# Modulation weights by contraction chunks, products slot by slot, and the vector tables ahead of the weight ring

## The chip, the cores and the metric

The kernel runs on one core of a Trainium2 chip. The metric is the time of one execution on the device, in microseconds (us). Five engines work side by side, each on its own list of instructions: TensorE (PE; its weight loads are shown as PEld), VectorE (DVE), ScalarE (ACT), GpSimd (POOL) and SyncE (SP). They meet at semaphores. SP and ACT also issue DMA transfers; in the profile SP's transfers stand under queue q1 and ACT's under q10, and both are carried out by the same 16 DMA engines.

## What is computed

One inference step of a two-layer backbone for two groups of 128 tokens (g = 0, 1), all in float32. Cut to what bears on the change:

```python
def _modulation(cond, w, b):              # w: 1024 x 6144
    m = jax.nn.silu(cond) @ w + b
    return jnp.split(m[:, None, :], 6, axis=-1)
...
for l in range(DEPTH):                    # DEPTH = 2
    sh1, sc1, g1, sh2, sc2, g2 = _modulation(cond, p['ada_w'], p['ada_b'])
    h = _rmsnorm(x, norm1) * (1 + sc1) + sh1
    proj = h @ p['w_in']                  # input projection, 3232 columns
    ...                                   # three mixer branches, merge, output projection
    x = x + g1 * mix
    x = x + g2 * _moe(_modulate(x, norm2, sh2, sc2), p)   # 32 experts, top 4
```

The condition has two rows, one for each group of tokens, so the modulation is a product of 2 rows with a 1024 x 6144 matrix in each layer.

## The kernel before

**The ring.** The weights of a layer's front (everything ahead of the experts) are packed on the host into 32 positions of up to 128 partitions x 4096 float32 (2 MB). Position `pos` is loaded into ring slot `pos % 6`. Positions 0 to 5 of layer 0 are loaded by `load_early` in a setup block, those of layer 1 at the end of layer 0. All others are loaded by SP in the order of their positions. SP waits, for each one, until the position that lay in the slot before has been used up: `consumed(pos)` names the semaphore and its value. PE waits in `arrived(pe, pos)` until a position has landed.

**The modulation** takes 12 positions: 0 to 3 (round r = 0: shift and scale of sub-layer 1), 15 to 18 (r = 1) and 25 to 28 (r = 2), in `S_ADA = (0, 15, 25)`. `ada_products(r, bank)` makes 32 matmuls, each of the 128 x 32 padded condition `cT[:, k, :]` with 512 columns of weights. Four of them, j = 0 to 3, go into four strips of 32 partitions of one PSUM bank and run side by side; k runs over the eight chunks of the contraction. The profile shows two records for a matmul. `front[S_ADA[r] + j]` holds all eight chunks of 512 columns, so each k needs all four slots. The bank is then copied to `msb[r]` (by DVE in round 0, by ACT in rounds 1 and 2), transposed by PE, and `modulation` on DVE makes the scale `A1` from it.

**The start of a layer, by engine.** PE: `norm(0, 7)` (L529), the modulation products (L538), four transposes (L545), and then the input projection, whose first position is 4. Its first unit (tokens of group 0) waits chunk by chunk for `h_dve0`, its second unit (group 1) for `h_act0`. DVE: waits for the vector table, then the scaling of x by the norm, some preparation, the copy L1205, the scale, and its half of the modulate (L1215), for group 0. ACT: the root of the norm (L912), two small activations on the vector table (L925, L926), seven loads (L931 twice, L916 four times, L937), and its half of the modulate (L944), for group 1. SP: refills of the ring.

**The vector tables** are `vec` (128 x 146, biases, norms and the like) and `row` (one row of 864, copied to all partitions). `load_vectors` loads them; in layer 0 it stands between the slots 3 and 4, at the end of layer 0 ahead of all six slots.

Later in the layer PE goes through the projection, the branches and the merge, and then through 13 and more passes of experts, whose weights SP loads into the ring slots and two further buffers as they come free.

Of the kernel before, what the change touches and what calls it, by code (L numbers as in the profile page):

```python
# [24 lines left out]
P = 128  # L25
D = 1024
KC = D // P
# [36 lines left out]
S_ADA = (0, 15, 25)  # L64
# [65 lines left out]
def build(nc, x_in, cond_in, consts, vecs, rows, front, lru_gate_w, router_w, exp_w1, exp_b1, exp_w2, exp_b2,  # L130
          cache_ckv, cache_krope, cache_dk, cache_dv, y_out, new_ckv, new_krope, new_lru, new_dk, new_dv):
    ctx = ExitStack()
    with ctx:
# [43 lines left out]
        def at(off, *dims):  # L177
# [8 lines left out]
            if len(dims) == 4:  # L186
# [102 lines left out]
        ada_mm, ada_sb, ada_tr, prep, mod_rdy = (sem(n) for n in  # L289
                                                 ("ada_mm", "ada_sb", "ada_tr", "prep", "mod_rdy"))  # L290
# [40 lines left out]
        def consumed(pos):  # L331

            for r in range(3):
                if S_ADA[r] <= pos < S_ADA[r] + 4:
                    return ada_mm, r + 1
            if pos in S_IN:
                return win_mm, 2 * (S_IN.index(pos) + 1)
            if pos in (S_QB, S_KVB):
                return p4_mm, {S_QB: 4, S_KVB: 10}[pos]
            return f_mm, max(f for f, m in enumerate(MERGE) if merge_slot(*m) == pos) + 1  # L340

        def arrived(eng, pos):

            if pos < RING:
                eng.wait_ge(early[pos], l * 16 + 16)
            else:
                eng.wait_ge(arr[pos % RING], 16 * (pos // RING))
            return ring[:, pos % RING, :]
# [20 lines left out]
        def load_vectors(eng, layer):  # L369

            eng.dma_start(vec[:, :], vecs[bass.ds(layer, 1), :, :].rearrange("o p n -> (o p) n")).then_inc(
                early_vec, 16)
            eng.dma_start(row[:, :], rows[bass.ds(layer, 1), :].broadcast_to((P, NR))).then_inc(early_row, 16)


        with nc.Block() as block:
            @block.sync
            def _(sp_):
                sp_.dma_start(xT[:, :, :], x_in).then_inc(s_set[2], 16)
                sp_.dma_start(cT[:, :, 0:G], cond_in).then_inc(s_set[0], 16)  # L380
                sp_.dma_start(cst[:, :], consts).then_inc(s_set[1], 16)
                for pos in range(RING):
                    load_early(sp_, 0, pos)
                    if pos == 3:
                        load_vectors(sp_, 0)
                sp_.wait_ge(s_set[1], 16)
                sp_.wait_ge(s_set[2], 16)

            @block.scalar
            def _(act):  # L390

                act.wait_ge(s_set[2], 16)
                nc.scalar.activation(sq[:, :, :], xT[:, :, :], ACT.Square)
                act.wait_ge(s_set[0], 16)
                nc.scalar.activation(cT[:, :, G:2 * G], cT[:, :, 0:G], ACT.Tanh, scale=0.5).then_inc(s_set[3], 1)

            @block.vector
            def _(dve):

                dve.wait_ge(s_set[3], 1)  # L400
                nc.vector.tensor_scalar(cT[:, :, G:2 * G], cT[:, :, G:2 * G], 0.5, 0.5, ALU.mult,
                                        ALU.add).then_inc(s_set[4], 1)
                dve.wait_ge(s_set[4], 1)
                nc.vector.tensor_tensor(cT[:, :, 0:G], cT[:, :, 0:G], cT[:, :, G:2 * G],
                                        ALU.mult).then_inc(s_set[4], 1)
                dve.wait_ge(s_set[4], 2)
                nc.vector.memset(cT[:, :, G:32], 0.0).then_inc(s_set[4], 1)


        with nc.Fori(0, L) as l:  # L410
            with nc.Block() as block:
# [109 lines left out]
                def _(pe):  # L521
# [3 lines left out]
                    def norm(i, bank):  # L525
                        for k in range(KC):
                            if i == 1:
                                pe.wait_ge(sq_rdy, k + 1)
                            last = mm(ps[:, bank, 0:NT], ones, sq[:, k, :], start=k == 0, stop=k == KC - 1)  # L529
                        last.then_inc(nrm_mm[i], 1)  # L530

                    norm(0, 7)
                    def ada_products(r, bank):

                        slots = [arrived(pe, S_ADA[r] + j) for j in range(4)]
                        for k in range(KC):
                            for j in range(4):
                                last = mm(ps[32 * j:32 * j + 32, bank, :], cT[:, k, :],  # L538
                                          slots[j][:, k * 512:(k + 1) * 512], start=k == 0, stop=k == KC - 1)
                        last.then_inc(ada_mm, 1)  # L540

                    def ada_transposes(r, bank):
                        pe.wait_ge(ada_sb, r + 1)
# [57 lines left out]
                    for n, (kind, w) in enumerate((("tok", 512), ("tok", 160), ("feat", 512), ("feat", 512),  # L601
# [3 lines left out]
                        slot = arrived(pe, S_IN[n])[:, 0:KC * w].rearrange("p (k n) -> p k n", n=w)  # L605
                        for half in range(2):
# [7 lines left out]
                            if kind == "tok":  # L614
                                for k in range(KC):
                                    if u == 0:
                                        pe.wait_ge(h_v[0], k + 1)
                                    if u == 1:
                                        pe.wait_ge(h_a[0], k + 1)
                                    last = mm(ps[:, bank, 0:w], hT[:, k, half * P:(half + 1) * P],  # L620
                                              slot[:, k, :], start=k == 0, stop=k == KC - 1)
                            else:
                                for c in range(2):
                                    for k in range(KC):
                                        ch = 2 * half + c
                                        last = mm(ps[:, bank, c * NT:(c + 1) * NT],  # L626
                                                  slot[:, k, ch * P:(ch + 1) * P], hT[:, k, :],
                                                  start=k == 0, stop=k == KC - 1)
# [70 lines left out]
                    for u in range(12):  # L699
# [8 lines left out]
                        if u < 8:  # L708
# [3 lines left out]
                               stop=True).then_inc(s_mm, 1)  # L712
                        else:
                            for c in range(2):
                                r = slice(64 * c, 64 * c + 64)
                                mm(ps[:, 2 + c, 0:128], b[r, 0:128], b[r, 256:384], start=True, stop=True)
                            for c in range(2):
                                r = slice(64 * c, 64 * c + 64)
                                last = mm(ps[:, 2 + c, 128:384], b[r, 128:256], b[r, 384:640], start=True,
                                          stop=True)  # L720
# [8 lines left out]
                        for n in range(3):  # L729
                            last = tr(ps[:, 4, n * P:(n + 1) * P], probs[u % 2][:, 0, n * P:(n + 1) * P], ident)  # L730
# [8 lines left out]
                        if u < 8:  # L739
                            if u % 2 == 0 and u:  # L740
                                pe.wait_ge(om_ev, u // 2)
                            r = slice(64 * (u % 2), 64 * (u % 2) + 64)
# [4 lines left out]
                               stop=True).then_inc(pv_mm, 1)  # L747
                        else:
# [3 lines left out]
                            else:  # L752
# [5 lines left out]
                               stop=True).then_inc(pv_mm, 1)  # L758
# [11 lines left out]
                    for k in range(KC):  # L770
# [3 lines left out]
                        last = mm(ps[c, 1, 0:NT], rw[:, k, :], hT[:, k, :], start=k < 4, stop=k >= 4)  # L774
# [12 lines left out]
                    for g in range(G):  # L787
                        last = mm(ps[:, 1, 256 + g * N_EXP:256 + (g + 1) * N_EXP], lpart[:, g * P:(g + 1) * P],
                                  cst[:, C_FOLD:C_FOLD + N_EXP], start=True, stop=True)
# [32 lines left out]
                    for g in range(G):  # L822
                        last = mm(ps[0:N_EXP, 0, g * P:(g + 1) * P], cmb[:, g, :], ident, start=True, stop=True)
# [76 lines left out]
                def _(act):  # L900
# [131 lines left out]
                              scale=0.5).then_inc(f_ac, 1)  # L1032

                    def modulation(r, bank):
                        act.wait_ge(ada_mm, r + 1)
                        A(msb[r], ps[:, bank, :], ACT.Copy).then_inc(ada_sb, 1)

                    merge_gates(8)
# [16 lines left out]
                    for u in range(12):  # L1055
                        act.wait_ge(nm_v, u + 1)
                        j = u % 2
                        if u < 8:
                            for n, c in enumerate((slice(0, 128), slice(128, 384))):
                                last = A(probs[j][:, 0, c], ps[:, 2 + j, c], ACT.Exp, bias=nm[:, j, n:n + 1],  # L1060
                                         accum_out=sums[:, j, n:n + 1])
                        else:
                            for n, c in enumerate((slice(0, 128), slice(128, 384))):
                                for m in range(2):
                                    e = 2 * n + m
                                    last = A(probs[j][:, m, c], ps[:, 2 + m, c], ACT.Exp, bias=nm[:, j, e:e + 1],
                                             accum_out=sums[:, j, e:e + 1])
# [31 lines left out]
                    for g in range(G):  # L1099
                        last = A(exl[:, g, :], lgt[:, g, :], ACT.Exp, bias=nv1[:, g:g + 1])  # L1100
# [33 lines left out]
                def _(dve):  # L1134
# [66 lines left out]
                                                   in1=vec[:, nrm:nrm + 8][:, :, None].broadcast_to((P, KC, G)),  # L1201
                                                   op0=ALU.add, op1=ALU.mult).then_inc(mod_rdy, 1)

                    dve.wait_ge(ada_mm, 1)
                    V.tensor_copy(msb[0], ps[:, 0, :]).then_inc(ada_sb, 1)  # L1205
                    modulation(0, 3)

# [19 lines left out]
                    for g in range(G):  # L1227
# [4 lines left out]
                        last = V.tensor_tensor_reduce(out=spare[:, g, 384:640], in0=kv, in1=kv, scale=1.0, scalar=0.0,  # L1232
                                                      op0=ALU.mult, op1=ALU.add, accum_out=ss[:, 2 + g:3 + g])
# [4 lines left out]
                    for g in range(G):  # L1238
# [3 lines left out]
                        last = V.scalar_tensor_tensor(out=kv, in0=kv, scalar=ss[:, 2 + g:3 + g],  # L1242
                                                      in1=row[:, R_KVA:R_KVA + KV_LORA], op0=ALU.mult, op1=ALU.mult)
# [10 lines left out]
                    for j in range(4):  # L1254
                        for c in range(RC):
                            w = vec[:, V_CW + 4 * j + c:V_CW + 4 * j + c + 1]
                            o = xr[:, c, :].rearrange("p (g n) -> p g n", g=G)
                            if j == 0:
                                last = V.tensor_scalar(o, xpad[:, c, :, 0:P], w, vec[:, V_CB + c:V_CB + c + 1],
                                                       ALU.mult, ALU.add)  # L1260
                            else:
                                last = V.scalar_tensor_tensor(out=o, in0=xpad[:, c, :, j:j + P], scalar=w, in1=o,
                                                              op0=ALU.mult, op1=ALU.add)
# [49 lines left out]
                    for g in range(G):  # L1313
                        last = scaled(q_tok[:, g, :, :], MLA_H, QK, ss[:, 8 * g:8 * g + 8], row[:, R_QN:R_QN + QK],
                                      float(QK) ** -0.5)
                        if g == 1:
                            link(last)
                            last = rotate(axes(q_tok[:, 1, :, NOPE:QK], 8), MLA_H, 8, cosm, sinm)
# [124 lines left out]
                    for u in range(12):  # L1443
                        j = u % 2
# [347 lines left out]
```

## Time and profile before

| | |
|---|---|
| time, median of 3 runs | 1726.78 us (1723.65 to 1728.42) |
| profiled execution | 1727.04 us, span 1725.4 us |
| PE busy | 1559.3 us (90%) |
| DVE busy | 571.2 us (33%) |
| ACT busy | 260.4 us (15%) |
| DMA | 545.81 MB, mean 316 GB/s |
| largest groups | L846 (experts) 368.7 us, L866 (experts) 186.6 us, L659 (merge) 171.4 us |

The span runs from the first to the last instruction. Busy times of different engines overlap. The granted clock of TensorE is given as a share of 2.4 GHz: 1.00 is that level, 0.50 is 1.2 GHz. A line number is that of the kernel before, unless the text says otherwise; in the changed kernel the same code stands one to two lines further up or down.

### The profile page before, as it was taken

The numbers are of one execution on the slowest core, as the hardware profiler recorded it, in microseconds if no ns is written. First come the engines' busy times: TensorE is split into PE (matmuls) and PEld (weight loads), VectorE is DVE, ScalarE is ACT, GpSimd is POOL, SyncE is SP. The second block draws the span as 40 slices with busy tenths as digits, with TensorE's granted clock in tenths as the row PEclk, the third lists the DMA queues.
The fourth block names the chain that finished last, engine by engine and source line by source line (L and its number), as shares of the span: only waits on it lengthen the run. The fifth ranks groups of instructions, "written<-read, shape, count | busy, mean of one in ns | idle before, by whom it ended". The sixth has DMA issues, their size and how long they took to land. (4 is left out here: it accounts for less than half of the span.)

```text
span 1725.4 us, 20291 instructions
## 1 busy us (share of the span) xinstructions
PE 1559.3 (90%) x8058; PEld 909.8 (53%) x8058; DVE 571.2 (33%) x1453; ACT 260.4 (15%) x583; POOL 3.8 (0%) x6
## 2 busy tenths in 40 slices
PE   4999999989889979796979999999899899797968
PEld 2756788754444444332447567887644444353424
DVE  2368336353611211111134583263445111121112
ACT  2044222030000000000021341220300000010001
POOL 0000000000000000000000000000000000000000
PEclk8999999999999989898989999999999999898979
DMA  9643622948999999999957347138479999999995
GB/s 376 255 183 137 281 99 98 378 165 326 421 431 418 415 431 411 421 430 431 388 212 297 150 153 292 62 141 341 202 294 411 430 420 412 431 413 421 431 429 219
DMA packets 48706, 545.81 MB, mean 316 GB/s; under 512 B 12704, under 2 KB 13472, under 8 KB 15584
## 3 DMA queue, kind: packets, MB, share of 16 engines
q1 hardware_dynamic: 39488, 539.95, 75.4%
q10 hardware_dynamic: 9120, 4.53, 1.0%
q8 instruction: 64, 1.05, 0.2%
q14 instruction: 34, 0.28, 0.0%
HBM read 542.06 MB, written 2.40 MB: 316 GB/s over the span
## 5 line engine op out<-in xcount | busy, mean ns | idle before, releaser
L846 PE MATMUL ps<-ring,arena 128*64 128x512 f32 (+2 forms) x1696 | 368.7, 634 | 39.2 <-DMA ring<-exp_w_dram 33.1
L846 PEld LDWEIGHTS ps<-ring,arena 128*64 128x64 f32 (+2 forms) x1696 | 117.8, 135 | 260.9 <-issue 259.4
L866 PE MATMUL ps<-ring,arena 128*64 128x512 f32 (+2 forms) x672 | 186.6, 657 | 28.5 <-DMA arena<-exp_w_dram 28.5
L659 PE MATMUL ps<-hT,ring 128*128 128x256 f32 x768 | 171.4, 379 | 0.0
L659 PEld LDWEIGHTS ps<-hT,ring 128*128 128x128 f32 x768 | 144.1, 190 | 19.4 <-issue 1.0
L866 PE MATMUL ps<-arena 128*32 128x512 f32 (+1 forms) x384 | 123.0, 676 | 28.2 <-DMA ring<-exp_w_dram 28.2
L659 PE MATMUL ps<-arena,ring 128*128 128x256 f32 x640 | 144.6, 380 | 2.9 <-ACT arena L1052 1.6
L846 PE MATMUL ps<-arena 128*32 128x512 f32 (+1 forms) x416 | 123.7, 651 | 7.3 <-DMA ring<-exp_w_dram 7.3
L659 PEld LDWEIGHTS ps<-arena,ring 128*128 128x128 f32 x640 | 118.8, 190 | 19.0 <-issue 2.7
L620 PE MATMUL ps<-ring,hT 128*128 128x512 f32 (+1 forms) x320 | 123.1, 546 | 1.9 <-DVE hT L1215 1.9
L807 PEld LDWEIGHTS ps<-arena 128*128 128x128 f32 x928 | 108.2, 192 | 25.1 <-issue 19.2
L807 PE MATMUL ps<-arena 128*128 128x128 f32 x928 | 115.3, 278 | 3.9 <-DVE arena L1541 3.9
L1114 ACT ACTIVATE arena<-arena 128x512 f32<-128x512 f32 x27 | 17.0, 631 | 662.2 <-DVE arena L1650 662.2
L866 PEld LDWEIGHTS ps<-ring,arena 128*64 128x64 f32 (+2 forms) x672 | 55.9, 140 | 107.7 <-issue 107.7
L1548 DVE TENSOR_TENSOR arena<-arena 128x256 f32<-128x256 f32 x27 | 11.5, 425 | 279.5 <-PE ps L846 279.4
L1662 DVE COPY arena<-ps 128x512 f32<-128x512 f32 x27 | 18.7, 692 | 250.5 <-PE ps L866 250.5
L874 PE MATMUL ps<-arena 128*128 128x256 f32 x432 | 100.0, 385 | 0.0
L874 PEld LDWEIGHTS ps<-arena 128*128 128x128 f32 x432 | 80.2, 190 | 30.6 <-issue 20.8
L620 PEld LDWEIGHTS ps<-ring,hT 128*128 128x128 f32 x320 | 58.6, 194 | 64.9 <-issue 63.6
L1650 DVE TENSOR_SCALAR arena<-ps 128x512 f32<-128x512 f32 x27 | 18.7, 691 | 182.2 <-PE ps L846 182.2
L866 PEld LDWEIGHTS ps<-arena 128*32 128x32 f32 (+1 forms) x384 | 32.2, 133 | 72.9 <-issue 72.9
L846 PEld LDWEIGHTS ps<-arena 128*32 128x32 f32 (+1 forms) x416 | 33.3, 131 | 54.2 <-issue 54.2
(282 smaller groups left out, 1391.8 us busy)
## 6 DMA issues: line engine op xcount, KB each, us to landing
ring<-exp_w_dram SPq DMA_DIRECT2D x146, 2048.0 KB, 16.0
ring<-front_dram SPq DMA_DIRECT2D x58, 2048.0 KB, 8.5
arena<-exp_w_dram SPq DMA_DIRECT2D x49, 2048.0 KB, 16.7
ring<-front_dram SPq DMA_DIRECT2D x2, 1152.0 KB, 15.7
ring<-front_dram SPq DMA_DIRECT2D x2, 1024.0 KB, 17.7
ring<-front_dram SPq DMA_DIRECT2D x2, 640.0 KB, 22.8
xT<-x_in_dram SPq DMA_DIRECT2D x1, 1024.0 KB, 4.9
arena<-lru_gate_w_dram ACTq DMA_DIRECT2D x4, 256.0 KB, 6.2
```

Source lines behind the costliest of these rows:

```text
L620: last = mm(ps[:, bank, 0:w], hT[:, k, half * P:(half + 1) * P], slot[:, k, :], start=k == 0, stop=k == KC - 1)
L659: last = mm(out, slot[:, k, cols], src[:, k, :], start=k == 0, stop=k == nk - 1)
L807: last = mm(ps[:, 2 + k // 4, (k % 4) * P:(k % 4 + 1) * P], X2[:, g, k * P:(k + 1) * P], S_s[:, g, :], start=g == 0, stop=g == 1)
L846: last = mm(ps[c, h, :], xTg[:, 4 * part + k, c], w[i][:, k, h * 512:(h + 1) * 512], start=False, stop=True, skip_group_check=True)
L866: last = mm(ps[c, 2 + h, :], actT[:, f, c], w[i][:, f, h * 512:(h + 1) * 512], start=f == 0, stop=f == 3)
L874: last = mm(ps[:, 4 + k // 2, (k % 2) * NT:(k % 2 + 1) * NT], O_s[:, k * P:(k + 1) * P], SCT[:, :], start=first and k % 2 == 0, stop=True, ...
L1114: A(sig_s, gate_s, ACT.Sigmoid, scale=ALPHA).then_inc(sig_a, 1)
L1548: V.tensor_tensor(SC_s.rearrange("p g (i w) -> p g i w", i=n), S_s.rearrange("p g (i w) -> p g i w", i=n), cwT[:, :, cols][:, :, :, None]. ...
L1650: V.tensor_scalar(gate_s, ps[:, 0, :], LIMIT, None, ALU.min).then_inc(gate_v, 1)
L1662: V.tensor_copy(O_s[:, 512:1024], ps[:, 3, :]).then_inc(o_v, 1)
```

## The change

Each modulation position now holds two chunks of the contraction for all 2048 columns of the round, instead of eight chunks for 512. `ada_products` waits for one position, makes the eight matmuls of its two chunks, counts `ada_mm` up and goes on to the next, so that `consumed` frees the four positions one after the other. The engines that read the bank wait for four counts per round. In the setup block the vector tables are loaded ahead of the six slots. The number and the shapes of all instructions stay the same, and so does the order of the matmuls.

```diff
@@ consumed
             for r in range(3):
                 if S_ADA[r] <= pos < S_ADA[r] + 4:
-                    return ada_mm, r + 1
+                    return ada_mm, 4 * r + pos - S_ADA[r] + 1
@@ setup block, SP
+                load_vectors(sp_, 0)
                 for pos in range(RING):
                     load_early(sp_, 0, pos)
-                    if pos == 3:
-                        load_vectors(sp_, 0)
@@ PE
                     def ada_products(r, bank):
-                        slots = [arrived(pe, S_ADA[r] + j) for j in range(4)]
                         for k in range(KC):
+                            if k % 2 == 0:
+                                slot = arrived(pe, S_ADA[r] + k // 2).rearrange("p (k n) -> p k n", k=2)
                             for j in range(4):
                                 last = mm(ps[32 * j:32 * j + 32, bank, :], cT[:, k, :],
-                                          slots[j][:, k * 512:(k + 1) * 512], start=k == 0, stop=k == KC - 1)
-                        last.then_inc(ada_mm, 1)
+                                          slot[:, k % 2, j * 512:(j + 1) * 512], start=k == 0, stop=k == KC - 1)
+                            if k % 2:
+                                last.then_inc(ada_mm, 1)
@@ ACT (rounds 1 and 2), DVE (round 0)
-                        act.wait_ge(ada_mm, r + 1)
+                        act.wait_ge(ada_mm, 4 * r + 4)
-                    dve.wait_ge(ada_mm, 1)
+                    dve.wait_ge(ada_mm, 4)
@@ host
-            front[S_ADA[r] + j] = blocks(a["ada_w"], (4 * r + j) * 512, 512)
+            front[S_ADA[r] + j] = blocks(a["ada_w"][:, 2 * j * P:2 * (j + 1) * P], r * 2048, 2048)
```

On PE, at the start of a layer, the products stood behind one wait for four slots (`slot0_early` to `slot3_early` are the semaphores of the first four positions):

```order
L538 MATMUL ps<-ring,cT 32x512 [waits slot2_early,slot3_early,slot1_early,slot0_early]
L538 MATMUL ps<-ring,cT 32x512 x31
L545 MATMUL ps<-cst,arena 128x128 [waits ada_sb]
L545 MATMUL ps<-cst,arena 128x128 x3
L620 MATMUL ps<-ring,hT 128x512 [waits h_dve0,slot4_early]
L620 MATMUL ps<-ring,hT 128x512 [waits h_dve0] x7
L620 MATMUL ps<-ring,hT 128x512 [waits h_act0] x8
```

The same place of PE's list in the changed kernel:

```order
L539 MATMUL ps<-ring,cT 32x512 [waits slot0_early]
L539 MATMUL ps<-ring,cT 32x512 x7
L539 MATMUL ps<-ring,cT 32x512 [waits slot1_early]
L539 MATMUL ps<-ring,cT 32x512 x7
L539 MATMUL ps<-ring,cT 32x512 [waits slot2_early]
L539 MATMUL ps<-ring,cT 32x512 x7
L539 MATMUL ps<-ring,cT 32x512 [waits slot3_early]
L539 MATMUL ps<-ring,cT 32x512 x7
L547 MATMUL ps<-cst,arena 128x128 [waits ada_sb]
```

The matmuls have kept their places; three waits stand among them now.

In SP's setup block the order of the loads was and is, as a piece of the difference:

```order
 L381 DMA cst<-consts_dram 128x866
-L367 DMA ring<-front_dram 128x4096 x4
 L371 DMA vec<-vecs_dram 128x146
 L373 DMA row<-rows_dram 128x864
-L367 DMA ring<-front_dram 128x4096
+L367 DMA ring<-front_dram 128x4096 x5
 L367 DMA ring<-front_dram 128x1280
```

The two tables have moved ahead of the four modulation positions.

On ACT nothing has moved. This is its list at the start of a layer, from its first preparation to its half of the modulate, in the kernel before (the waits on other queues' loads are of no account here):

```order
L931 DMA arena<-lru_gate_w_dram 64x16x64
L916 DMA arena<-cache_ckv_dram 128x256
L916 DMA arena<-cache_krope_dram 128x32
L916 DMA arena<-cache_dk_dram 128x512
L916 DMA arena<-cache_dv_dram 128x512
L937 DMA rw<-router_w_dram 128x8x32
L944 ACTIVATE hT<-hT,modT,A 128x128 [waits hraw0,mod_rdy]
L944 ACTIVATE hT<-hT,modT,A 128x128 [waits hraw0] x7
```

The first of these rows stands twice in the list. The innermost number is the contiguous piece in float32, so a gate-weight load is 64 x 16 pieces of 256 bytes.

## Rows read from the trace of the kernel before

**Rows 1.** The page's head.

```profile
span 1725.4 us, 20291 instructions
```

**Rows 2.** Waits of PE, 0 to 320 us: in total, times, longest.

```profile
PE ps L538 <- DMA ring<-front_dram: 13.1, 1, 13.1
```

**Rows 3.** Timeline of layer 0, PE and DVE: start, length, engine, line, operation.

```profile
8.99 5.26 PE L529 MATMUL ps<-arena,cst 128*128 128x256 f32 x16 [8.99 <-PEq L376]
27.32 9.70 PE L538 MATMUL ps<-ring,cT 128*32 128x512 f32 x64 [13.07 <-DMA ring<-front_dram]
27.45 0.17 DVE L1146 SCALAR_TENSOR_TENSOR sp<-vec 128x8 f32<-128x8 f32 x1 [19.00 <-DMA vec<-vecs_dram]
...
39.45 20.01 PE L620 MATMUL ps<-ring,hT 128*128 128x512 f32 x64 [0.97 <-DVE hT L1215]
...
48.29 0.69 DVE L1224 COPY arena<-ps 128x512 f32<-128x512 f32 x1 [7.19 <-PE ps L620]
...
55.15 0.69 DVE L1224 COPY arena<-ps 128x512 f32<-128x512 f32 x1 [6.17 <-PE ps L620]
```

**Rows 4.** SP's issues, then us to landing of slot 0, `row`, slot 5.

```profile
2.56 1.88 SPq L367 DMA_DIRECT2D ring<-front_dram  x4
5.02 0.71 SPq L373 DMA_DIRECT2D row<-rows_dram  x1
5.77 1.17 SPq L367 DMA_DIRECT2D ring<-front_dram  x2
...
ring<-front_dram SPq DMA_DIRECT2D x1, 2048.0 KB, 10.1
...
row<-rows_dram SPq DMA_DIRECT2D x1, 432.0 KB, 23.5
...
ring<-front_dram SPq DMA_DIRECT2D x1, 640.0 KB, 29.1
```

**Rows 5.** Timeline of layer 1's start: PE, ACT's issues, DVE's two copies.

```profile
896.81 7.07 PE L538 MATMUL ps<-ring,cT 128*32 128x512 f32 x64
...
899.09 1.49 ACTq L931 DMA_DIRECT2D arena<-lru_gate_w_dram  x2
...
900.73 0.55 ACTq L916 DMA_DIRECT2D arena<-cache_ckv_dram  x1
...
915.16 0.69 DVE L1224 COPY arena<-ps 128x512 f32<-128x512 f32 x1 [7.19 <-PE ps L620]
...
922.03 0.69 DVE L1224 COPY arena<-ps 128x512 f32<-128x512 f32 x1 [6.17 <-PE ps L620]
```

**Rows 6.** Stretches: length, PE, PEld, DVE, ACT, POOL busy, granted clock, DMA share, GB/s.

```profile
19.50:27.00 7.50, 0.00 (x0) 0.00 (x0) 0.00 (x0) 0.00 (x0) 0.00 (x0) 0.50 0.98 414
27.00:32.60 5.60, 5.28 (x28) 1.53 (x32) 5.08 (x15) 1.79 (x3) 0.00 (x0) 0.50 1.03 439
...
39.50:42.60 3.10, 3.10 (x4) 1.40 (x5) 1.60 (x7) 3.08 (x8) 0.00 (x0) 0.50 0.97 396
```

**Rows 7.** Timeline of ACT's queue in layer 0.

```profile
28.04 1.55 ACTq L931 DMA_DIRECT2D arena<-lru_gate_w_dram  x2
29.76 4.88 ACTq L916 DMA_DIRECT2D arena<-cache_ckv_dram  x1
```

**Rows 8.** Packets, MB, share by queue: 30-31, 32-34 (two), 32-34.6 (q10), 35-36 us.

```profile
q1 hardware_dynamic: 28, 0.46, 107.4%
...
q1 hardware_dynamic: 132, 0.75, 89.7%
q10 hardware_dynamic: 127, 0.03, 7.1%
...
q10 hardware_dynamic: 365, 0.09, 15.8%
...
q10 hardware_dynamic: 986, 0.25, 130.8%
```

**Rows 9.** SP's queue from 39.4 to 56 us: packets, MB, share.

```profile
q1 hardware_dynamic: 562, 6.21, 88.8%
```

## Prediction

> **What bounds the kernel now.** I read four views, in this order: the page's span, the waits of PE, the timeline of the first 60 us of each layer, and the DMA packets by queue in short stretches. The profiled execution took 1727.04 us, 1.6 more than its span [rows 1]; the median of the runs is 0.3 less, so I add the sum to 1727.0 and take 0.3 off. PE works almost without a pause in the front of both layers. Its only wait for a weight there is the one in the change's place: 13.1 us ahead of the first modulation products, ended by the fourth slot [rows 2]. After it come 9.7 us of products, and 2.4 us after their end the input projection starts at 39.45 [rows 3]. Everything later in the layer hangs on PE, and the expert loads are issued as PE frees buffers, so a shift of the first projection moves the whole rest of the run one for one.
>
> Ring slot 0 (2 MB) is issued at 2.56 and lands after 10.1, at 12.7; the fourth lands at 27.2, when PE starts, so slots come some 4.8 us apart. The two vector tables follow and are in at 28.5 (5.02 + 23.5): 1.3 us of the DMA's time. Slot 5 is in at 35.6 (6.5 + 29.1) [rows 3, 4].
>
> **What the products gain.** The tables now lie ahead of slot 0: slots 0 to 3 land 1.3 later, at 14.0, 18.7, 23.6 and 28.5. PE's norm ends at 14.25 [rows 3]. Each slot's quarter of the products is 1.77 us at full clock (7.07 for all 64 records in layer 1) [rows 5] and 3.5 at half. After PE's idle stretch the granted clock was 0.50, the 1.2 GHz level, both from 19.5 to 27 and from 27 to 32.6 while it worked [rows 6]; with bursts and pauses in turn I take half for the last. It ends at 28.5 + 0.2 (for a cost named below) + 3.5 = 32.2 where all products ended at 37.0. The same 2.4 us of copy, transposes and modulation follow, and the projection could start at 34.6, 4.8 earlier. At full clock it would be 6.5. The DVE's preparation, which waited for the vector table until 27.45 [rows 3], goes into its idle time. The three added PE waits per round cost nothing that I can see: in layer 1 the data are there, and the slot-wise waits only order what already ran in this order. Four products that run side by side now read one slot instead of four; no row prices that, and below nothing I see no reason for it; I take 0, and from above a doubling of each round's 7.07 us [rows 5], to which I give no weight, since the streams stay the same in number and length.
>
> **What the early release does.** This decides it, for me. SP refills ring slots 0 to 3 as soon as each quarter is done: in layer 0 the refills queue behind slot 5 from 16 us on instead of after all products (37.0), in layer 1 from 898.6 on instead of after 903.9. PE needs none of them sooner (it never waited for one). But the ACT queue issues seven small loads at this point: two gate-weight loads of 1024 rows of 256 bytes, four of 128 rows, and the router's of 1024 rows of 128 bytes, 3584 packets in all. ACT's own sequencer issues them, and behind them in program order stands its half of the first modulate, L944, for which PE waits in the second unit of the projection (h_act0).
>
> How the two queues share the engines is in the rows. The gate weights were issued at 28.04 [rows 7], and from 30 to 31 the engines moved only SP's queue, 28 packets in the us. From 32 to 34 they moved 132 of SP's and 127 of ACT's: one for one. From 35 on, with SP's queue empty, ACT's went at 986 per us [rows 8]. So ACT's small packets move at SP's packet rate as long as SP's queue holds anything. And the ACT sequencer felt it: its third load, issued at 29.76, took 4.88 us to issue [rows 7], in layer 1, with SP's queue empty, 0.55 [rows 5]. When it was through, some 127 to 365 of ACT's packets had moved (to 34.0 and to 34.6) [rows 8], so 2048 + 128 less those, 1811 to 2049, are what the queue holds. The router load, last of 3584, can then be issued only when 1535 to 1773 have moved. In the kernel before this was met within 2 us, because SP's queue had run empty before 35.
>
> Layer 0 after the change: in layer 1 the gate loads are issued 2.2 us after the norm [rows 5], so here at 14.25 + 2.2 = 16.5, for the vector table is in. Their first packets come 4 us later (28.04 to 32), at 20.5. To 33.4 they move at 28 per us, 361; beside slot 5's 128 rows another 128; beside the four refills' 4 x 128 rows another 512: 1001 in all. That costs SP's queue 3% (127 packets took 7.1% of 2 us, so 28 take 3.1% of one) [rows 8], 0.2 us on slot 3, 0.4 on slot 5. The refills took some 16 us from 39.4 [rows 9]; now they follow slot 5 at 36.0 and end at 52.0. SP's next refill waits for the projection's second unit, which waits for ACT: only now does SP's queue run dry. The missing 534 to 772 packets take 0.7 us, the router load is issued at 52.7, and the first of ACT's modulates is done 0.5 later. The second unit starts at 53.2; it starts after 10 us of idling, so at half clock like the first one, which took 8.84 from its start to its copy (39.45 to 48.29). Its copy comes at 62.0 instead of 55.15 [rows 3]. **Layer 0: +6.9 us**, with the 4.8 of gain lost in it.
>
> Layer 1: all six slots are there, the products end at 903.9 as before and the first unit's end does not move (915.0, just ahead of its copy at 915.16). SP's queue is busy from about 900.4 (1.8 after the first release at 898.6), just as ACT's first packets start. The refills' 16 us and 0.4 for the sharing end at 916.8; 512 of ACT's packets moved beside them, 1023 to 1261 are missing, 1.2 us at layer 0's 986 per us; the load is issued at 918.0, the second unit starts at 918.5 and is copied 8.84 later, at 927.3, against 922.03 [rows 5]. **Layer 1: +5.3 us.** Of this 2.0 (8.84 less the 6.87 between the two copies) is the half clock: a gap of 2.4 us with four transposes in it had brought it back to 0.50 at 39.5 [rows 3, 6], and this one is 3.5. Rounds 1 and 2 of the modulation lie inside dense PE work, with no ACT loads of many rows near; nothing there.
>
> **Sum:** 1727.0 + 6.9 + 5.3 - 0.3 = 1739.
>
> **The ratio against the page.** The rows give one ACT packet for one of SP's. The Trainium skill, "DMA: Bandwidth & Descriptors", section "Queues, rings and completion order", says an engine drains a whole packet, typically 9 to 17 descriptors, from one queue's ring before it switches to the next. If that held for ACT's short rows against single long rows of SP's, ACT's 1654 packets would be through in about 3.5 to 6.6 us and the time would be that of rival 1. The 132 against 127 speak against it.
>
> **Rivals.**
> 1. *ACT's queue is not held up* (it holds more than I worked out, or the sharing is better once both queues are full). Then only the gain of 4.8 in layer 0 is left: 1722. For it: I have one blocked issue to go by, and layer 1 of before shows none. Against it: the 4.88 us and the 0.55. It decides from the point where the router load is issued before 43.5, when the first unit's work ends. With a full clock in the last burst it is 1720.
> 2. *A load is let in when its beginning fits*, so the router's needs no more room than a small one: 511 to 749 packets moved. In layer 0 this is at 36 to 46, the second unit starts at 43.3 to 46.2, and its copy is 4.8 to 0.1 early; in layer 1 it is at 917.0, +4.3. Sum -0.5 to +4.2, about 1729. For it: the second gate load, which made 2048, went in at once before any packet had moved.
> 3. *Slower than my sum*: the slowest of the 16 engines decides when the load is in, and a single late one costs 2 to 4 us in each layer: 1745 and more.
>
> **How the numbers follow.** Main case 0.60, with 1735 to 1743 as its own range (the clock of the second units, 0 to 4 us less, and the end of the refills, 2 us either way); rival 1 0.18, rival 2 0.14, rival 3 0.08. A measurement of this kernel can tell about 0.3%, 5.2 us, from no change. The main case and rival 3 are slower, with 0.02 of rival 2; the rest of rival 2 is within; rival 1 stands at the bound, 0.08 faster and 0.10 within. So faster 0.08, same 0.22, slower 0.70. The range reaches down into rival 1 and up to rival 3: 1722 to 1745, with 0.17 left out.
>
> **What the profile after would show.** Right: the products' line in four bursts that begin at 14.3, 18.7, 23.6 and 28.7; ACT's loads issued from 16.5; the third and later ones taking several us each to issue; the router load issued near 52.7 and 918.0; PE idle ahead of the second unit, ended by ACT's modulate, some 10 us and 3.5 us; one ACT packet for one of SP's from 21 to 50. Wrong: ACT's modulate at 34 and 905.8 with no idle in the projection (rival 1), or only in layer 1 (rival 2).

## The result: 1.0% slower, and the profile after

The changed kernel takes 1743.65 us in the median of five runs (1742.26 to 1745.54), against 1726.78: 16.9 us more, a ratio of 1.0103 with a 95% interval of 1.0091 to 1.0116. The profiled execution took 1745.5 with a span of 1743.7, 18.3 more than in [rows 1].

The waits of PE over the whole run (in total, times, longest) show what was traded:

```profile
PE ps L622 <- ACT hT L946: 16.7, 2, 9.4
...
PE ps L539 <- DMA ring<-front_dram: 6.8, 3, 3.0
```

The one wait of 13.1 us in [rows 2] has become three of 6.8 in all; a new one on ACT's half of the modulate stands in both layers, 9.4 and 7.3 us.

This is the timeline of layer 0 with the rows of all engines mixed, to be held beside [rows 3, 4, 7]. The bracket at the end of a row is the engine's idle time before it and what ended it; for an issue (ACTq, SPq) the second number is how long the issuing took:

```profile
15.33 1.92 PE L539 MATMUL ps<-ring,cT 128*32 128x512 f32 x16
...
17.48 77.82 SPq L417 DMA_DIRECT2D ring<-front_dram  x8
17.61 1.54 ACTq L933 DMA_DIRECT2D arena<-lru_gate_w_dram  x2
...
18.90 1.92 PE L539 MATMUL ps<-ring,cT 128*32 128x512 f32 x16 [1.65 <-DMA ring<-front_dram]
19.32 30.26 ACTq L918 DMA_DIRECT2D arena<-cache_ckv_dram  x1
...
28.80 3.23 PE L539 MATMUL ps<-ring,cT 128*32 128x512 f32 x16 [2.14 <-DMA ring<-front_dram]
...
34.48 8.80 PE L622 MATMUL ps<-ring,hT 128*128 128x512 f32 x16 [0.96 <-DVE hT L1217]
...
49.75 0.56 ACTq L918 DMA_DIRECT2D arena<-cache_krope_dram  x1
...
51.61 0.39 ACTq L939 DMA_DIRECT2D rw<-router_w_dram  x1
52.11 3.18 ACT L946 ACTIVATE hT<-hT,modT,A 128x128 f32<-128x128 f32 x8 [33.07 <-issue]
52.66 14.51 PE L622 MATMUL ps<-ring,hT 128*128 128x512 f32 x48 [9.38 <-ACT hT L946]
...
62.86 0.69 DVE L1226 COPY arena<-ps 128x512 f32<-128x512 f32 x1 [18.86 <-PE ps L622]
```

The projection starts 5.0 us earlier (34.48 for 39.45), which is the gain that the change can give. Then ACT's third load takes 30.26 us to issue (such a long issue is called a hold below), the four behind it follow between 49.75 and 52.0, and only then can ACT begin its modulate at 52.11. Nothing but its own issuing held it: "33.07 <-issue". The second copy is 7.7 us later than before.

Layer 1, beside [rows 5]:

```profile
903.87 7.07 PE L539 MATMUL ps<-ring,cT 128*32 128x512 f32 x64
...
906.02 49.95 SPq L417 DMA_DIRECT2D ring<-front_dram  x7
906.14 1.50 ACTq L933 DMA_DIRECT2D arena<-lru_gate_w_dram  x2
...
907.80 14.65 ACTq L918 DMA_DIRECT2D arena<-cache_ckv_dram  x1
...
923.33 1.84 ACTq L918 DMA_DIRECT2D arena<-cache_dk_dram  x1
925.25 1.43 ACTq L918 DMA_DIRECT2D arena<-cache_dv_dram  x1
...
927.83 13.84 PE L622 MATMUL ps<-ring,hT 128*128 128x512 f32 x48 [7.34 <-ACT hT L946]
...
937.36 0.69 DVE L1226 COPY arena<-ps 128x512 f32<-128x512 f32 x1 [16.14 <-PE ps L622]
```

The products start 7.1 us later than before, the second copy comes 15.3 later: 8.3 are lost at the same place. The 3.0 that are left to the 18.3 of the span come after this copy, and the merge and the experts lie there.

The packets by queue (q1 is SP's, q10 ACT's) from 22 to 49.6 us, the same from 911 to 922.4, and then from 51 to 52:

```profile
q1 hardware_dynamic: 944, 10.92, 96.6%
q10 hardware_dynamic: 944, 0.24, 3.9%
...
q1 hardware_dynamic: 422, 4.52, 94.7%
q10 hardware_dynamic: 422, 0.11, 4.2%
...
q10 hardware_dynamic: 657, 0.17, 73.6%
```

944 against 944, and 422 against 422: the sharing is one packet for one, whatever their sizes. ACT's 944 packets carried 0.24 MB in 27.6 us; with SP's queue nearly empty it moved 657 in one.

### The profile page after: what moved, and what is told of

It reads as the page before. It is cut to its first block and busy times, and to the rows that moved or that the text cites. A ratio compares the mean times of both kernels' runs of the same rounds, so it can differ in the third digit from the quotient of the medians.

```text
span 1743.7 us, 20281 instructions
## 1 busy us (share of the span) xinstructions
PE 1559.5 (89%) x8058; PEld 911.3 (52%) x8058; DVE 571.0 (33%) x1453; ACT 260.1 (15%) x583; POOL 3.8 (0%) x6
## 5 line engine op out<-in xcount | busy, mean ns | idle before, releaser
L622 PE MATMUL ps<-ring,hT 128*128 128x512 f32 (+1 forms) x320 | 127.3, 559 | 18.6 <-ACT hT L946 16.7
```

## The experiments

Ten kernels, each compared with the kernel before on the same chip. Each edit is made in the changed kernel unless it says otherwise.

**The tables alone** (in the kernel before):

```diff
+                load_vectors(sp_, 0)
                 for pos in range(RING):
                     load_early(sp_, 0, pos)
-                    if pos == 3:
-                        load_vectors(sp_, 0)
```

> The kernel before with the vector tables alone moved ahead of the six slots. Theory A (ACT's short-row loads are held up by SP's early refills, and ACT's half of the modulate stands behind them): with the old release there are no early refills, so ACT's third load is issued when SP's queue runs dry near 35, the router load by 37, before the modulation is ready; the four slots land 1.3 us later and the rest moves with them: 1728, +1 us. Rival B (the tables ahead are what does it, since ACT's loads are issued 10 us earlier): the second copy of the projection in layer 0 is some 8 us late: 1735.

Measured: 1725.66 us, ratio 1.0001 (0.9986 to 1.0015). The tables are not the cause. ACT's third load was held here too:

```profile
17.84 1.55 ACTq L930 DMA_DIRECT2D arena<-lru_gate_w_dram  x2
19.56 13.15 ACTq L915 DMA_DIRECT2D arena<-cache_ckv_dram  x1
...
35.72 0.40 ACTq L936 DMA_DIRECT2D rw<-router_w_dram  x1
...
39.39 3.18 ACT L943 ACTIVATE hT<-hT,modT,A 128x128 f32<-128x128 f32 x8 [20.12 <-DVE A L1199]
```

Without early refills SP's queue empties near 35, all is issued by 36, and ACT still waits for the scale afterwards. A hold of 13 us costs nothing there.

**The slot-wise products alone** (the tables back between slots 3 and 4, the reverse of the diff above):

> The changed kernel with the vector tables back between slots 3 and 4. Theory A: ACT's loads are issued near 28 instead of 17.6, but SP's refills are already queued, so ACT is let go at the same moment, when SP's queue runs dry near 50; layer 1 is as in the changed kernel: 1742 to 1745, within 2 us of the changed kernel. Rival B: layer 0's 8 us are gone, 1735.

Measured: 1746.09 us, ratio 1.0111 (1.0096 to 1.0127). The third load was issued at 29.91 and took 19.82 us: it ended at 49.7, as in the changed kernel (49.6), though it began 10.6 us later. So the end of the hold is set by SP's queue, not by when ACT starts, nor by how many of ACT's packets have moved (693 here, 954 in the changed kernel). The time is a us above the range expected.

**Release at the end of a round:**

```diff
-                    return ada_mm, 4 * r + pos - S_ADA[r] + 1
+                    return ada_mm, 4 * r + 4
```

> The changed kernel, but SP refills the four slots of a round only when the whole round is done. Theory A: in layer 0 all four refills are queued at 32.2, before slot 5 is through, so SP's queue still does not run dry until 51 and the 8 us remain; in layer 1 the refills come after ACT's loads as in the kernel before and its 8 us are gone: 1734 to 1736, +8. Rival C (the new layout of the products itself or their split is slow): both layers keep their loss, 1743.

Measured: 1725.52 us, ratio 0.9994 (0.9971 to 1.0017). The loss is gone in layer 1, as expected, and against the expectation in layer 0 as well:

```profile
18.65 14.80 ACTq L918 DMA_DIRECT2D arena<-cache_ckv_dram  x1
...
32.90 64.92 SPq L417 DMA_DIRECT2D ring<-front_dram  x9
...
37.30 0.40 ACTq L939 DMA_DIRECT2D rw<-router_w_dram  x1
37.80 3.19 ACT L946 ACTIVATE hT<-hT,modT,A 128x128 f32<-128x128 f32 x8 [19.44 <-issue]
```

The third load was through at 33.45 (18.65 + 14.80), half a us after the refills were issued and before any of them ran. From 34 to 38 ACT's queue moved 1477 packets to SP's 123, so the refills that were issued at 32.90 did not hold it. I had counted a queued refill as a busy queue from the moment of its issue. ACT was ready at 37.8, before PE needed it. The ten runs spread widely, from 1717.4 to 1737.2.

**ACT's loads behind its modulate:**

```diff
-                    act.wait_ge(lruw_zero, 1)
-                    for j in range(2):
-                    ...                                   # the seven loads
                     def modulate(i, scale, shift):
                         ...
                     modulate(0, A1, 0)
+                    act.wait_ge(lruw_zero, 1)
+                    for j in range(2):
+                    ...                                   # the seven loads
```

> The changed kernel with ACT's seven loads behind its half of the modulate in ACT's program order; nothing else changed. Theory A: PE's wait for ACT in the second unit is gone in both layers, and the gain of the slot-wise products is left, 4.8 to 5.5 us in layer 0, 0 in layer 1: 1721 to 1722, the second copy of layer 0 near 50.3. The loads themselves land by 57, long before PE asks for them near 82. Rival C (layout, split or clock): still above 1740.

Measured: 1722.55 us, ratio 0.9976 (0.9964 to 0.9987), faster than both kernels, and 21.1 us less than the changed one (1743.65). The hold is still there, but nothing stands behind it:

```profile
34.83 0.49 ACT L933 ACTIVATE hT<-hT,modT,A 128x128 f32<-128x128 f32 x1 [15.85 <-DVE A L1203]
...
36.71 12.54 ACTq L918 DMA_DIRECT2D arena<-cache_ckv_dram  x1
...
50.77 0.69 DVE L1227 COPY arena<-ps 128x512 f32<-128x512 f32 x1 [6.18 <-PE ps L622]
```

The second copy is 4.4 us ahead of the one before. The kernel before was at 1726.17 on this chip, so the gain over it is 3.6 us by the medians and 4.1 by the ratio (2 to 6 by its interval).

**Long rows in ACT's loads** (same bytes, but for the zeros: 64 x 16 pieces of 256 bytes become 64 rows of 8 KB, twice; the router's 1024 pieces become 128 rows of 1 KB, by an edit of the same kind that is not shown, like the packing on the host):

```diff
-                        src = lru_gate_w[bass.ds(l, 1), bass.ds(j, 16, step=2), :, :]
-                        act.dma_start(lruw[64 * j:64 * j + 64, :, 64 * j:64 * j + 64],
-                                      src.rearrange("o b c e -> c (o b) e")).then_inc(ld_lruw, 16)
+                        src = lru_gate_w[bass.ds(l, 1), 64 * j:64 * j + 64, :]
+                        act.dma_start(lruw[64 * j:64 * j + 64, :, :].rearrange("p b n -> p (b n)"),
+                                      src.rearrange("o p n -> (o p) n")).then_inc(ld_lruw, 16)
```

> The changed kernel with ACT's three short-row loads in long rows: the gate weights zero-padded on the host (2 loads of 64 rows of 8 KB instead of 1024 of 256 bytes) and the router's in 128 rows of 1 KB, so 768 packets instead of 3584 and 0.5 MB more. Order, releases and everything else as in the changed kernel. Theory A (the queue holds a limited number of rows, and ACT's rows pass only at SP's packet rate): no issue is held up, ACT's modulate starts as soon as the scale is there near 34, PE's wait for it is gone in both layers: 1721 to 1723. Rival D (ACT's third load is held as long as SP's queue has anything, whatever its rows; the runs so far fit that too): ACT is let go only near 50 and 922, 1743.

Measured: 1729.92 us, ratio 1.0024 (1.0010 to 1.0038). Rival D falls: no issue was held, the last one was made at 20.0. But the time I expected was missed by 7 us, and the same rule of sharing has a part in it. The timeline, and then the packets from 22 to 32 us:

```profile
20.04 0.39 ACTq L939 DMA_DIRECT2D rw<-router_w_dram  x1
...
37.34 3.64 PE L539 MATMUL ps<-ring,cT 128*32 128x512 f32 x16 [4.31 <-DMA ring<-front_dram]
...
60.77 0.69 DVE L1226 COPY arena<-ps 128x512 f32<-128x512 f32 x1 [6.17 <-PE ps L622]
...
DMA packets 230, 2.42 MB, mean 242 GB/s; under 512 B 32, under 2 KB 32, under 8 KB 32
...
q1 hardware_dynamic: 113, 1.59, 66.6%
q10 hardware_dynamic: 117, 0.83, 32.7%
```

Again one for one, but ACT's packets are 8 KB now and take a third of the engines' time, just when PE waits for slots 2 and 3. The last quarter of the products starts at 37.34 instead of 28.80. Short rows starve ACT; long rows starve SP. The sharing is only a part of this loss, though. In the same 10 us the changed kernel moved 4.28 MB at 428 GB/s, 4.21 of them SP's. Two thirds of that would be 2.85 MB for SP, and it got 1.59: all traffic together had fallen to 242 GB/s. What slowed it beside these loads no run shows.

**The control** for the edit of the fourth run, in the kernel before:

> The kernel before with ACT's seven loads behind its half of the modulate, the control for that edit. Theory A: in the kernel before the loads were issued before ACT was needed, so nothing changes: 1725 to 1728, and the 4 us that the changed kernel with the same edit gained come from the slot-wise products. Rival E: the edit gains by itself (fewer rows beside slots 4 and 5): 1722.

Measured: 1727.16 us, ratio 1.0006 (0.9993 to 1.0019). So the 4 us come from the slot-wise products and the tables, not from moving the loads. A single profile is a weaker witness than the medians here: in this one, of the fastest run (1722.29), the second copy came at 52.86, 2.3 us ahead of the one before, though only the place of ACT's loads had changed.

**Release after the third quarter:**

```diff
-                    return ada_mm, 4 * r + pos - S_ADA[r] + 1
+                    return ada_mm, 4 * r + max(pos - S_ADA[r] + 1, 3)
```

> The changed kernel with the release of the round's first three slots put off to the end of the third quarter (layer 0 near 26 instead of 17 to 26, layer 1 some 5.3 us after the products' start instead of 1.8). Theory A: in layer 0 SP's queue still never runs dry before 50 and ACT is held as before, +8 us in the second copy less the 4.8; in layer 1 ACT's third load is issued 4 us after the products' start, ahead of the first refill packet, so nothing is held and the 8 us of layer 1 are gone: 1733 to 1736. If it is the number of early refills rather than the timing that counts, both layers keep their loss, 1743.

Measured: 1735.53 us, ratio 1.0063 (1.0042 to 1.0084), as expected. In layer 0 the refills are issued at 26.02 and the hold is back, in layer 1 it is not:

```profile
18.39 31.13 ACTq L918 DMA_DIRECT2D arena<-cache_ckv_dram  x1
...
26.02 40.86 SPq L417 DMA_DIRECT2D ring<-front_dram  x6
...
62.07 0.69 DVE L1226 COPY arena<-ps 128x512 f32<-128x512 f32 x1 [16.84 <-PE ps L622]
...
905.37 0.55 ACTq L918 DMA_DIRECT2D arena<-cache_ckv_dram  x1
...
907.02 36.55 SPq L417 DMA_DIRECT2D ring<-front_dram  x7
```

The medians split the loss by layer: 10.0 us between this run and the one with the release at the end for layer 0's hold (the second copies, 62.07 and 51.97, are 10.1 apart), and 8.1 us to the changed kernel for layer 1's. Each of the two has some 4 us of uncertainty: this median is of four runs from 1730.75 to 1739.67, and the profiled one, the fastest, ended only 4.1 us after the other profile, since 4.4 of the 10.1 had been made up before layer 1 began.

**One gate load ahead:** `gate_load(1)` and the router's load behind the modulate, the rest ahead.

> The changed kernel with one gate-weight load and the four small loads ahead of ACT's modulate, the other gate load and the router's behind it. Theory A with a queue that holds about 2048 rows (128 on each of 16 engines): 1024 + 4 x 128 rows fit, no issue ahead of the modulate is held, ACT's modulate starts near 34: 1721 to 1723. If what holds is any load behind a short-row one while SP's queue is full, the second issue already takes 30 us: 1743.

Measured: 1723.50 us, ratio 0.9977 (0.9964 to 0.9990). The time is as expected, the reason not quite: in layer 0 the first small load behind the gate load went in at once (0.58), and the other three took 4.87, 4.21 and 3.44 us to issue, which ended at 31.1, 3 us before ACT was needed; in layer 1 the last took 10.27 and cost PE a wait of 0.85 us. So much less than 2048 rows already hold an issue back.

**The small loads ahead, all three of many rows behind:**

> The changed kernel with only the four small loads (4 x 128 rows) ahead of ACT's modulate and both gate loads and the router's behind it. It asks how little is held up: with one gate load ahead, each small load behind it already took 3.4 to 4.9 us to issue in layer 0, and the last one 10.3 us in layer 1. If rows in the queue are what holds (more than about 1100), none of the four takes over 0.6 us, ACT's modulate starts with the scale in both layers: 1721 to 1723. If a small load too is held behind another while SP's queue is full, ACT is late by 4 to 10 us in layer 1 and the time is 1725 or more.

Measured: 1722.00 us, ratio 0.9977 (0.9967 to 0.9988). None of the four took over 0.45 us, in either layer. 512 rows do not hold an issue back.

**Without the early tables, and with the loads behind:**

> The changed kernel with ACT's loads behind its modulate, as the fastest one so far, but with the vector tables back between slots 3 and 4: what the early tables are worth once ACT is not held. The slots land 1.3 us earlier, so the products end near 31; DVE starts its preparation at 27.5 and ends it at 33.4, as in the kernel before, so its copy of the products comes at 33.4 instead of 32.5. Expected: +1 us against the run with the tables ahead, 1723 to 1724, and the second copy of layer 0 near 52. If the tables were the source of the gain: 1727.

Measured: 1725.94 us, ratio 0.9998 (0.9988 to 1.0009), 2 us above the expectation. The DVE does end its preparation last:

```profile
32.66 0.29 DVE L1190 TENSOR_REDUCE lam<-lprod 128x2 f32<-128x128 f32 x1
32.87 0.68 DVE L1209 COPY arena<-ps 128x512 f32<-128x512 f32 x1
...
52.58 0.69 DVE L1228 COPY arena<-ps 128x512 f32<-128x512 f32 x1 [6.18 <-PE ps L623]
```

The second copy is at 52.58, 1.8 us after that of the fourth run (0.4 at the copy of the products, the rest in the first unit at half clock). The medians differ by 3.4. The 1.6 between is not placed: in the profile of the run with the small loads ahead the second copy came at 52.58 as well, with the tables ahead, and its median is 1722.0. The part of the tables is thus somewhere between 0 and 3.4 us. And without the early tables no gain over the kernel before is shown (1725.94 against 1725.98 on the same chip), nor had the tables alone given one: only both together came out clearly faster.

## Why the prediction came out, point by point

**The gain at the start of the projection, 4.8 us, was right.** The bursts began at 15.3, 18.9, 23.8 and 28.8, the last took 3.2 with the clock at 0.59 from 29 to 32, and the projection started at 34.48 (I had 34.6). With the hold out of the way the median gains 3.6 to 4.1 us (fourth run), for the products and the tables together.

**The mechanism was right and is shown, not only argued.** Taking away what stands behind the loads gives back 21 us; releasing late gives back 18; the tables alone do nothing. Loads of the same kind with fewer packets are not held. The ratio of one packet for one, which I took from 132 against 127 in [rows 8], is exact over 944. In the order of the records from 22 to 49.6 us the two queues' counts, over all 16 engines together, are never more than 7 apart, so they take turns row by row. In the choice between that row and the Trainium skill ("DMA: Bandwidth & Descriptors", section "Queues, rings and completion order", a whole packet of 9 to 17 descriptors at a turn), the row was right: no run shows a turn of more than one row.

**The size was too small: +12.2 forecast, +16.9 measured.** The 1743.65 lies just above the main case's own range of 1735 to 1743. By the terms:
- Layer 0, "+6.9": measured 7.7. The refills and the release of ACT were right to 1 us (the second unit starts at 52.66, I had 53.2). The unit itself took 10.2 us to its copy and not 8.84, since its half clock lasted longer, 6.1 us (the clock was 0.50 on average from 52.66 to 58.8) for some 3.4 in the kernel before:

```profile
52.70:56.00 3.30, 3.30 (x4) 1.47 (x5) 0.00 (x0) 3.28 (x8) 0.00 (x0) 0.50 0.84 227
56.00:59.00 3.00, 3.00 (x5) 1.21 (x4) 0.00 (x0) 2.08 (x3) 0.00 (x0) 0.53 0.03 9
59.00:62.80 3.80, 3.80 (x11) 1.66 (x10) 0.00 (x0) 0.00 (x0) 0.00 (x0) 1.00 0.00 0
```

- Layer 1, "+5.3": measured 8.3, counted from the start of its products. Here the step that failed is "the missing packets take 1.2 us". All but the last few rows of the refills were through at 923.6, which is 916.5 in the time of the kernel before, as forecast (916.8). The third load was let go at 922.45, but the four behind it needed until 927.2 (1.84 and 1.43 us for the two of 2 KB rows), 3.6 us after the refills and not 1.2. With 0.2 more until PE starts, that makes the second unit 2.3 us later than forecast; the unit's own length is the other 0.7 of the 3.0. Half of the size missed is in this term. The number of packets does not explain it: when the second of these loads was through, at 925.17, 1938 of ACT's had moved. What was late is one of the 16 engines, which still carried out SP's last rows, one after the other, until 926.4. The same stands in layer 1 of the fourth run, first the issue, then the packets from 912.9 to 915.1, and, last, those of the changed kernel from 924 to 926.4:

```profile
912.34 3.26 ACTq L918 DMA_DIRECT2D arena<-cache_dk_dram  x1
...
q10 hardware_dynamic: 1074, 0.34, 81.5%
q1 hardware_dynamic: 3, 0.02, 5.4%
...
q1 hardware_dynamic: 4, 0.02, 5.7%
```

  A share of 5.4% or 5.7% is less than one engine of 16 (6.25%), and yet a load of 128 rows took 3.26 us to issue. So it looks as if the queue of the latest engine held the issue. That is not shown, since the records do not name the engine.
- Between the two layers 0.6 comes back (7.7 late at the second copy, 7.1 at layer 1's products).
- The rest, 3.0 in the span and 1.6 by the medians, comes later. PE's waits for expert weights are 111.0 us in this profile and 103.2 in the one before; but they are 110.8 in the fourth run, which is faster than both, so I put nothing of it down to the change. From layer 1's second copy to the end the twelve profiles took 802.7 to 806.3 us. The two kernels with both holds are the longest there (806.3 each), but the third and the eighth run, with no loss in the median, are close (805.8 and 805.6), and the one before took 803.4. It stays open.

**A step that was wrong without harm to the sum:** that ACT's third load goes when 127 to 365 packets have moved. It was held until 954 had moved in layer 0. In all kernels where it was held behind both gate loads, its issue ended shortly before the end of SP's queued loads, within some 3 us of it, with 256 to 974 of ACT's packets moved. What the queue waits for within that I cannot tell from these runs; I only worked out wrongly what it holds (2048 rows or so, where 1024 and 128 already held the next issue in the eighth run). That my sum did not notice was luck: the router's load needed SP's queue to be empty by either account. The third run did notice.

**The rivals.** Rival 1 (no hold) did not occur; with the loads moved behind, so that the hold costs nothing, the fourth run took 1722.6, the time given for that rival (1722). Rival 2 did not occur either: the second unit started at 52.66 and not by 46.2. Rival 3 (one late engine, 1745 and more) is not excluded as a part of the size: one engine ended SP's rows 2 to 3 us after the others in both layers, at 54.0 and 926.4. In layer 0 that cost nothing, for the router's load was through at 52.0; in layer 1 it falls where 2.3 us are missing from my sum.

## What to carry to other kernels

Ask of a buffer that is freed earlier what its refill will share the DMA engines with: if nothing needs the refill sooner, it can only get in the way. Two queues share packet by packet here, so ACT's short rows beside SP's of 16 KB got 29 rows per us (289 from 22 to 32 us), and a sequencer whose issue is held stops, with everything behind the load in program order. So put compute that others wait for ahead of loads of many short rows, and issue these where a long hold has cover.

## What the runs showed of the hardware that I had not expected

- The sharing counts packets and not bytes, in both directions: 256-byte rows got 2% of the bytes (0.24 of 11.2 MB), 8 KB rows got a third of them (0.83 of 2.42 MB) while all traffic fell from 428 to 242 GB/s; together that delayed a slot by 8.5 us.
- Refills issued half a us before ACT's hold ended did not prolong it (third run: at 32.90, the hold ended at 33.45); issued at 26.02 they did, to 49.5 (seventh run).
- 1024 rows and 128 more in ACT's queue were enough to hold the next issue for 4.9 us, while two loads of 1024 rows each go in one after the other in 1.5 us when they come first.
- SP's last rows of a stretch were left to one late engine for 2 to 3 us, and with only that engine behind, the issue of a load of 128 rows still took 3.26 us (fourth run, layer 1).
